# Two token halves in turn for each weight tile, in whole units of a projection

## What is computed

```python
xn = rmsnorm(x, ln_g)
proj = xn @ w_in                       # 1024 -> 11264 columns: q, k, v, z_a, x_b, z_b, g_a, g_b
...
o_a = group_norm(ret, gn_g).astype(x.dtype) * jax.nn.silu(z_a)      # retention, 4 heads
...
o_b = h.astype(x.dtype) * jax.nn.silu(z_b)                          # conv and RG-LRU, 1536 wide
merged = jax.nn.sigmoid(g_a) * (o_a @ w_a) + jax.nn.sigmoid(g_b) * (o_b @ w_b)
return x + merged @ w_o, S_new, conv_new, h_last
```

## Time and profile before

| | |
|---|---|
| runs | 1936.89, 1937.38, 1938.43 us |
| median | 1937.38 us |
| span of the profiled execution, first to last instruction | 1935.6 us |
| PE busy | 1916.6 us (99%), 13184 matmuls |
| PEld busy | 1795.2 us (93%), 13184 loads |
| DVE busy | 1181.8 us (61%) |
| ACT busy | 742.3 us (38%) |
| HBM | 122 GB/s over the span |

### The profile page before, as it was taken

One profiled execution on the slowest core, in us unless ns is written; L12 is line 12 of the kernel. 1 busy time (PEld: TensorE's weight loads), 2 busy tenths in 40 slices (PEclk: granted clock), 3 DMA queues, 4 the chain that ended last, 5 costly groups with the idle time before them and its releaser, 6 DMA issues.

```text
span 1935.6 us, 32128 instructions
## 1 busy us (share of the span) xinstructions
PE 1916.6 (99%) x13184; PEld 1795.2 (93%) x13184; DVE 1181.8 (61%) x2008; ACT 742.3 (38%) x1149; POOL 266.6 (14%) x375
## 2 busy tenths in 40 slices
PE   8999999999999999999999999999999999999998
PEld 7889898898899999999998988988988999999997
DVE  8765665565666887424486655656556678853345
ACT  5332322323336766422333223233223367754223
POOL 2220120120231200000031201202102422000000
PEclk9999999999999999999999999999999999999999
DMA  6434534453443333322255345534533533332222
GB/s 216 135 114 163 188 115 126 160 169 112 134 153 98 107 105 111 119 77 77 88 170 174 122 126 168 169 113 136 175 119 137 165 98 106 99 135 79 85 80 82
DMA packets 105856, 247.01 MB, mean 128 GB/s; under 512 B 10830, under 2 KB 51134, under 8 KB 105326
## 3 DMA queue, kind: packets, MB, share of 16 engines
q1 hardware_dynamic: 78590, 149.74, 24.8%
q0 software_dynamic: 26976, 95.22, 14.7%
q10 hardware_dynamic: 144, 0.00, 0.0%
HBM read 186.10 MB, written 49.12 MB: 122 GB/s over the span
## 4 chain that ended last, share of the span: by engine, by line
PE 87%; DVE 5%; ACT 4%; DVEq 1%; ACTq 1%; issue 1%; DMA 0%; SPq 0%
PE bank L1629 21%; PE bank L1631 21%; PE bank L1630 21%; PE bank L1699 5%; PE bank L1701 5%; PE bank L1700 5%; PE last L1717 2%; PE last L1699 1%; PE last L1701 1%; PE last L1700 1%; PE bank L1857 1%; DVE ct L1421 1%; PE sums L1734 1%; DVE w_lo L463 1%; DVE rr L1474 1%
## 5 line engine op out<-in xcount | busy, mean ns | idle before, releaser
L1629 PE MATMUL bank<-xn_hi,w_hi 128*128 128x296 f32 (+1 forms) x2432 | 727.4, 299 | 0.2
L1631 PE MATMUL bank<-xn_lo,w_hi 128*128 128x296 f32 (+1 forms) x2432 | 722.4, 297 | 0.0
L1630 PE MATMUL bank<-xn_hi,w_lo 128*128 128x296 f32 (+1 forms) x2432 | 721.4, 297 | 0.0
L1629 PEld LDWEIGHTS bank<-xn_hi,w_hi 128*128 128x128 f32 x2432 | 457.2, 188 | 5.8 <-issue 4.3
L1630 PEld LDWEIGHTS bank<-xn_hi,w_lo 128*128 128x128 f32 x2432 | 457.9, 188 | 0.4
L1631 PEld LDWEIGHTS bank<-xn_lo,w_hi 128*128 128x128 f32 x2432 | 456.8, 188 | 0.0
L463 DVE TENSOR_TENSOR w_lo<-w_raw,w_hi 128x1024 fp32r<-128x1024 f32 x245 | 300.3, 1229 | 186.2 <-ACT w_hi L455 179.0
L455 ACT ACTIVATE w_hi<-w_raw 128x1024 fp32r<-128x1024 f32 x245 | 257.7, 1055 | 353.6 <-DMA w_raw<-in_w_units 349.1
L1629 PE MATMUL bank<-oa_hi,w_hi 128*128 128x296 f32 (+1 forms) x512 | 153.7, 300 | 0.0
L1630 PE MATMUL bank<-oa_hi,w_lo 128*128 128x296 f32 (+1 forms) x512 | 151.9, 297 | 0.0
L1631 PE MATMUL bank<-oa_lo,w_hi 128*128 128x296 f32 (+1 forms) x512 | 151.7, 296 | 0.0
(11 more groups left out here) (286 smaller groups left out, 3080.6 us busy)
## 6 DMA issues: line engine op xcount, KB each, us to landing
w_raw<-in_w_units SPq DMA_DIRECT2D x215, 512.0 KB, 3.6
S<-in_state_ret POOLq DMA_DIRECT2D x64, 512.0 KB, 4.8
out_ret_s<-S POOLq DMA_DIRECT2D x64, 512.0 KB, 6.1
w_raw<-in_w_units SPq DMA_DIRECT2D x66, 256.0 KB, 3.3
vst<-v_scr SPq DMA_DIRECT2D x8, 512.0 KB, 4.0
out_ret_p<-Sp POOLq DMA_DIRECT2D x8, 512.0 KB, 6.1
v_scr<-vtok_hi SPq DMA_DIRECT2D x16, 160.0 KB
dec<-in_decay POOLq DMA_DIRECT2D x9, 264.0 KB, 5.1
```

The costliest lines, as they stand in the source:

```text
L1629: pe.matmul(ps, w_hi[:, slot, cols], x_hi, start=first, stop=False)
L1630: pe.matmul(ps, w_lo[:, slot, cols], x_hi, start=False, stop=False)
L1631: return pe.matmul(ps, w_hi[:, slot, cols], x_lo, start=False, stop=last)
```

## The change

For a call of `project` with both halves, the change waits for both banks first. Then it takes for each k and each of the three products the two halves in turn, with the same weight tile. The half signals come after the last matmul of each half, which are now the last two matmuls of the unit. Calls with one half go on as before.

```diff
--- before.py
+++ after.py
@@ -1643,6 +1643,21 @@
                 x_hi, x_lo = left or (xn_hi, xn_lo)
                 every = ph == "R" and 2 <= tile[1] < 4 or ph == "L" and tile[2] < 3
                 wait_unit(ph, l, it, i)
+                if which == (0, 1):
+                    columns = [slice(a, b) for a, b in (HALVES if every else cut(l))]
+                    for n in which:
+                        wait_bank(pe, ph, l, it, (tile, n))
+                    ps = [psum_of(ph, (tile, n))[:, 0:columns[n].stop - columns[n].start] for n in which]
+                    for k in range(KT):
+                        cols = slice(k * P, k * P + P)
+                        for weight, x, first, last in ((w_hi, x_hi, k == 0, False), (w_lo, x_hi, False, False),
+                                                       (w_hi, x_lo, False, k == KT - 1)):
+                            for n in which:
+                                ins = pe.matmul(ps[n], weight[:, i % RING, cols], x[:, k, columns[n]],
+                                                start=first, stop=last)
+                                if last:
+                                    done(ph, (tile, n), ins)
+                    return
                 for n in which:
                     a, b = (HALVES if every else cut(l))[n]
                     name = (tile, n)
```

## The result

The change costs 7.5 us. The median is 1944.86 us (1944.29 to 1945.69) against 1937.38 us, a ratio of 1.0037 with a 95% interval of 1.0026 to 1.0049. The span of the profiled execution went from 1935.6 to 1943.0 us, +7.4. The time lies in the forecast's range, 5 us above its centre, and on the side, slower, that was given 0.44.

A forecast was written before the change was run, and what follows sets the result against it. The prediction took PE's sequence of matmuls plus its few waits as the bound. Span 1935.6 + 0 + 1.2 + 0.2 + 1.1 = 1938.1 us, with the median 1.8 above: 1939.9 us; range 1934.5 to 1948.

The forecast's parts named there:

- slower: Whole kernel: a time above 1941.3 us, beyond the 0.2% a measurement can tell from no change; chance 0.44.
- the likeliest case, no measurable difference: Whole kernel: a time within 0.2%, 3.9 us, of the kernel before; chance 0.48.
- Loads and matmuls unchanged: PE's matmuls: none is removed and each keeps a weight load of its own; 13184 of each expected.
- The 31 us that a shared load would save: Changed units: 3120 x 10 ns saved if the second matmul of each pair needed no load; the prediction argued against it.
- I take 0 for the spacing: Matmuls of the changed units: the new order leaves their start-to-start spacing as it is, 0 us.
- The bound in the same paragraph: Spacing in changed units: 4128 x 0.9 - 2112 x 0.4 = +2.9 us if the new order is like the `project_first` stretches.
- Tile 2 of the first head, +1.2 us: Layer 0: half 0 also waits for the late bank, 3.3 us, of which three later waits absorb 2.1.
- Rival D: PE's clock is granted at its lower level at times; 1% of 846 us would be +8 us, 1948; chance 0.02.
- Tile 2 in layer 1, +0.2: First head, layer 1: the unit waits for the read of half 1's bank ending at 990.45, +0.2 us.
- RG-LRU and gate tiles, +1.1: Tile 2 of RG-LRU groups and following gate tiles: small waits for late ACT reads, +1.1 us (0.5 to 2).
- Later handover, 0: Half 0 is complete 3.26 us later for its readers; costed at nothing, or 0.46 us per head and group without cover.
- Rival A: All 130 changed units: crossing banks at every matmul costs time, 1942.8 us with +2.9, 1948.5 with +8.6; chance 0.27.

The follow-up runs named there:

- e2: The change's waits for both banks at each whole unit's start, but the 24 matmuls of half 0 first, then half 1's, as in the kernel before: 1942.41 us.
- e5: The kernel before, with the two high-weight products adjacent in whole units, so one matmul in three repeats a weight tile in the same bank: 1937.54 us.
- e6: The kernel before, with only tile 2 of the first head (both layers) waiting for both banks at its start: 1941.43 us.
- e12: The kernel before, with halves alternating and no repeated weight tile only in 43 whole 288-column units of layer 1 without late banks: 1936.99 us.
- e4: The change, but halves alternate per weight tile, three products on half 0 then three on half 1, as in `project_first`: 1943.49 us.
- e9: The change, with 36 more matmuls into an unused bank before the wait of tile 2 of the first head in layer 0: 1942.22 us.

## Why the prediction was right, and where it was not

The range held, and slower was given 0.44, but the likeliest case, no measurable difference, was not what happened. That the range held is in part luck: it reached up to 1948 for the price of crossing banks, which turned out to be nothing, and what filled it was a longer spacing of another cause and the clock. By the steps of the sum:

- **Loads and matmuls unchanged.** Right: 13184 each, and each repeated tile is loaded again. The 31 us that a shared load would save did not come.
- **"I take 0 for the spacing."** This is the larger term that failed. Measured: 4128 x 0.84 - 2112 x 0.20 = +3.0 us. The bound in the same paragraph, +2.9 if the new order is like the two stretches of `project_first`, had the right sign at both widths. I had set it aside because the two signs looked like noise. They are not noise: the first 41 spacings of the stretch at 930.81 take 5.60 us in each of six profiles (before, the change, e2, e5, e6, e12), and the mean over the changed units is 135.80 to 135.82 ns in the four of them that keep the old order at 296 columns (before, e2, e6, e12). That the bound lies so near is luck in part, since the order of `project_first` in whole units, e4, would give only 4128 x 0.63 - 2112 x 0.53 = +1.5 us.
- **Tile 2 of the first head, +1.2 us.** As a wait, right in each part: 3.3 us later (3.34 in e9), the three waits behind it gone (no idle time is listed for PE from 39 to 60 us in the change; 2.2 us absorbed, 2.1 forecast), +1.1 left in e9. Wrong in "the unit starts at 30.88 and ends at 30.88 + 6.52": it takes 8.38 us. What is missing is the clock: 5.07 - 3.34 = 1.7 us by the ends of the unit in the change and in e9.
- **Rival D, the clock, 0.02.** I argued against it from a clock row that reads full throughout, but the kernel it belongs to never leaves PE idle that long. The sum itself said that the idle time would grow from 1.7 to over 5 us. The Trainium skill, "TensorE: Matmul & The Clock Gate", section "HAM oscillation — how this bites in real kernels", describes the like for waits for transfers: a wait between groups of matmuls sends the clock back to the lower level, and the next group starts cold. The rows at 27 to 37 us agree for a wait for banks, 0.50 in the later part of the wait and for some 4 us of work after it. I cited the neighbouring section on cycling banks and passed over this one. What that section tells doesn't show here: the change crosses banks in every matmul of its units, and the clock row stays at 9 in every slice after the first. (The 846 us in changed units of that rival are 841 by the prediction's own two spacings, which changes nothing.)
- **Tile 2 in layer 1, +0.2.** Measured +0.44 in the change, +0.56 in e6. The lateness was right; the unit then starts 0.15 us after the release, where I took 0.05, and its first two matmuls take 0.34 us together and not 0.27.
- **RG-LRU and gate tiles, +1.1.** Right in the waits, a little high in sum. Less its spacing, tile 2 of the six groups ends 0.7 us later in all (0.8 forecast), that of the gate tiles 0.24 and 0.52 us (0.15 and 0.45), but the three units that give something back give 0.6 and not 0.3. What the slopes leave beside spacing and tile 2 of the first head is 3.0 - 3072 x 0.84 ns = 0.4 us in layer 0 from 58.0 on, and 0.4 us in layer 1, 0.8 together.
- **Later handover, 0.** Right: each against its own runs of the kernel before, e2, which hands half 0 over as before, costs 4.8 us and the change 7.5. The difference of 2.7 us is no more than the spacing.
- **Rival A** had the right sign and a fair size, 1942.8 us, but the wrong mechanism: crossing banks costs nothing (136.65 ns with it, 136.64 without). With the clock's 1.7 us added it would have given 1944.5, by luck.

The terms as measured: 1.1 + 1.7 (clock) + 3.0 (spacing) + 0.4 + 0.8 = 7.0, and 0.4 that this execution had before the first changed unit, 7.4 in all.

## What to carry to other kernels

A wait that makes TensorE idle for several us can be priced twice: by its length and by the matmuls behind it, which here ran at 1.2 GHz for another 4 us. Look for it in the granted clock by stretches of 2 us; in a slice of 48 us it hardly shows. If the wait can't be avoided, matmuls into a free bank can keep the clock (36 of them took 1.7 us off here, by the ends of the unit). And when an edit reorders thousands of matmuls, take a difference of half a nanosecond between two orders in the trace as a value and not as noise: for the same order at the same place it repeats.

## What the runs showed of the hardware

- The clock fell to its lower level during an idle time of some 5 us on TensorE in all eight profiles that had one at this place. It stayed full there after idle times of up to 1.7 us (five profiles), and with matmuls in the gap (e9). A long idle time is not the only occasion: in four of the fourteen profiles the clock was low from about 8 us on for 3 to 7 us, after idle times of 1.2 and 1.0 us in the change, and the kernel before kept it full after the same.
- At 296 columns of float32r the spacing of matmuls depends on the order in which operands are read, 135.8 to 136.65 ns in the mean and 134.3 to 137.4 by position in the kernel before, and not on a change of bank or on a repeated weight tile. At 288 columns it goes the other way, 132.8 to 132.3.
- A matmul that repeats the weight tile of the one before it has a load of its own, 188 ns (13184 loads for 13184 matmuls in the change).
- After the wait for both banks at 996.76 and 1714.96 the first matmul started 0.15 us after the end of the read that released it, and its first two spacings took 0.34 us and not 0.27, together some 0.2 us for each wait beside its length. After the wait in the middle of the unit in the kernel before it started 0.05 us after the earlier trace rows.
